# Three of eight output chunks finished on GpSimd, and eight stores in place of four

## The reference

```python
def rmsnorm(x, g):
    xf = x.astype(f32)
    y = xf * lax.rsqrt(jnp.mean(xf * xf, axis=-1, keepdims=True) + EPS)
    return y.astype(x.dtype) * g

def layer_step(x, ...):
    ...
    x = x + g1 * o
    x = x + g2 * hier_moe(modulate(rmsnorm(x, n2), sh2, sc2), ...)
    return x, new

    y_prompt = rmsnorm(xp, final_norm_g)
    y_sample = rmsnorm(xs, final_norm_g)
```

## Time and profile before

| | us |
|---|---|
| median of 3 runs | 781.53 (781.06 to 781.74) |
| span of the profiled execution, first to last instruction | 780.0 |
| TensorE busy | 740.1 (95%) |
| VectorE busy | 582.4 (75%) |
| ScalarE busy | 502.5 (64%) |
| GpSimd busy | 50.4 (6%) |
| last multiplication of the program ends | 770.60 |
| first of the eight scalings begins, the last ends | 772.93, 777.22 |
| first store issued, last store issued | 774.10, 777.25 |

### The profile page before, as it was taken

How to read it: one execution, slowest core, us unless ns; L and a number is a source line. 1 busy time by engine, 2 the same in 40 slices (tenths; PEclk the granted TensorE clock), 3 DMA queues, 4 the chain that set the end, 5 groups by cost and what they waited for, 6 DMA issues and landing times.

```text
span 780.0 us, 10973 instructions
## 1 busy us (share of the span) xinstructions
PE 740.1 (95%) x4020; PEld 573.8 (74%) x4020; DVE 582.4 (75%) x968; ACT 502.5 (64%) x834; POOL 50.4 (6%) x36
## 2 busy tenths in 40 slices
PE   4999999899999999999999999989999999999995
PEld 2557877458966788888768788755798788888874
DVE  3258386987565889999858746979766789998965
ACT  3049693584456877777746578557556887777852
POOL 0001342000000000000000125200000000000000
PEclk9999999999999999999999999999999999999998
DMA  9963034977238899999855112186741199999902
GB/s 366 425 244 109 11 124 155 424 274 289 103 116 350 317 377 356 363 366 381 312 232 184 55 55 70 67 355 235 287 149 55 55 328 376 378 364 376 368 20 84
DMA packets 33489, 186.26 MB, mean 239 GB/s; under 512 B 5136, under 2 KB 6288, under 8 KB 16400
## 3 DMA queue, kind: packets, MB, share of 16 engines
q1 hardware_dynamic: 33424, 185.42, 62.9%
HBM read 182.79 MB, written 2.62 MB: 238 GB/s over the span
## 4 chain that ended last, share of the span: by engine, by line
PE 77%; DVE 11%; ACT 7%; issue 4%; DMA 1%; DVEq 0%; ACTq 0%; SPq 0%
PE psum L877 23%; PE psum L906 11%; PE psum L1024 11%; PE psum L1226 5%; PE psum L991 4%; PE psum L707 3%; PE psum L929 3%; PE psum L855 2%; DVE att L2264 1%; PE psum L758 1%; PE psum L1196 1%; PE psum L743 1%; PE psum L1094 1%; ACT split L1419 1%; PE psum L890 1%
## 5 line engine op out<-in xcount | busy, mean ns | idle before, releaser
L2053 DVE TENSOR_TENSOR split<-ring,split 128x2048 fp32r<-128x2048 f32 x96 | 219.9, 2290 | 27.1 <-ACT split L1544 25.4
L1544 ACT CAST split<-ring 128x2048 fp32r<-128x2048 f32 x96 | 183.6, 1912 | 22.4 <-PE psum L906 14.5
L877 PE MATMUL psum<-split,y_hi 128*128 128x512 f32 x512 | 161.1, 396 | 0.4 <-ACT selT L1517 0.4
L877 PEld LDWEIGHTS psum<-split,y_hi 128*128 128x128 f32 x512 | 93.7, 188 | 18.7 <-issue 0.5
L877 PE MATMUL psum<-split,y_lo 128*128 128x512 f32 x256 | 100.2, 391 | 0.0
L1024 PE MATMUL psum<-ring_r,hT_hi 128*128 128x512 f32 x216 | 73.2, 393 | 0.0
L906 PE MATMUL psum<-split,hidT 128*128 128x512 f32 x256 | 69.7, 394 | 1.8 <-DVE hidT_lo L2058 1.8
L906 PEld LDWEIGHTS psum<-split,hidT 128*128 128x128 f32 x256 | 47.3, 188 | 14.1 <-DVE hidT_lo L2058 4.8
L877 PEld LDWEIGHTS psum<-split,y_lo 128*128 128x128 f32 x256 | 48.0, 188 | 10.4
L2495 POOL TENSOR_TENSOR ud<-const,da_hi 128x1024 fp32r<-128x1024 f32 x12 | 27.3, 2293 | 398.8 <-DVE da_lo L2154 391.3
L1024 PEld LDWEIGHTS psum<-ring_r,hT_hi 128*128 128x128 f32 x216 | 40.0, 188 | 9.0 <-issue 0.8
(11 more groups left out here) (314 smaller groups left out, 1426.3 us busy)
## 6 DMA issues: line engine op xcount, KB each, us to landing
ring<-in_w_gu SPq DMA_DIRECT2D x64, 1024.0 KB, 6.1
ring<-in_w_ada SPq DMA_DIRECT2D x40, 1024.0 KB, 7.0
ring<-in_w_down SPq DMA_DIRECT2D x32, 1024.0 KB, 6.2
ring<-in_w_rows SPq DMA_DIRECT2D x12, 1024.0 KB, 4.9
ring<-in_first SPq DMA_DIRECT2D x8, 1024.0 KB, 14.7
ring<-in_w_out SPq DMA_DIRECT2D x8, 1024.0 KB, 5.0
ring<-in_w_xbc SPq DMA_DIRECT2D x8, 800.0 KB, 9.2
par<-in_par SPq DMA_DIRECT2D x1, 1728.0 KB, 13.5
```

Source lines behind the costliest of these rows:

```text
L877: last = pe.matmul(dst, x[:, g, t, :], w[:, j, :], start=(t == 0 and i == 0), stop=(t == KD - 1 and i == 2))
L1544: act.copy(splits[unit_split(n)][:, 0, :], slot(key)).then_inc(raised("whi", l, p), 1)
L2053: tt(lo, slot(unit_key(l, p, n)), hi.bitcast(F32), ALU.subtract).then_inc(raised("wlo", l, p), 1)
```

## The change

ScalarE writes, for chunks 0, 1 and 2, x times the chunk's column of the gain into `hT`, one instruction behind each of these chunks' squares (`with_gain`). The final Exp writes `rstd` in SBUF and raises the bank's semaphore, as in layer 1. VectorE scales only the other five chunks, now with `rstd` as its factor. GpSimd waits for the bank's semaphore and multiplies the three prepared chunks by `rstd`, in place. SP issues eight stores of one chunk (192 KB) each, in the order 3, 4, 0, 5, 1, 6, 7, 2, each behind the wait for its chunk.

```diff
+LAST_POOL = (0, 1, 2)
+LAST_DVE = tuple(c for c in range(KD) if c not in LAST_POOL)
+LAST_OUT = (3, 4, 0, 5, 1, 6, 7, 2)
...
-            for c in range(0, KD, 2):
-                sp.wait_ge(*modulated(DEPTH, 0, c + 1))
-                sp.dma_start(a_out[0][:, c:c + 2, :], hT[:, c:c + 2, :]).then_inc(y_out, 16)
-            sp.wait_ge(y_out, 16 * KD // 2)
+            for c in LAST_OUT:
+                if c in LAST_POOL:
+                    sp.wait_ge(sig["hp"], LAST_POOL.index(c) + 1)
+                else:
+                    sp.wait_ge(sig["h"], KD + LAST_DVE.index(c) + 1)
+                sp.dma_start(a_out[0][:, c, :], hT[:, c, :]).then_inc(y_out, 16)
+            sp.wait_ge(y_out, 16 * KD)
...
+            def with_gain(c):
+
+                act.activation(hT[:, c, :], xT[:, c, :], ACT.Copy, scale=pcol[:, 2 * N_PROW + c:2 * N_PROW + c + 1])
+
...
                     act.activation(sq[:, c, :], xT[:, c, :], ACT.Square).then_inc(sig["sq"], 1)
+                    if l == DEPTH and c in LAST_POOL:
+                        with_gain(c)
...
-                if l in ROUNDED:
+                if l in ROUNDED or l == DEPTH:
                     act.activation(rstd, src[:, 0:TOK], ACT.Exp, scale=-0.5).then_inc(*was_read(key))
...
-                if l in ROUNDED:
+                if l in ROUNDED or l == DEPTH:
                     dve.wait_ge(*taken(key))
...
                 if l == DEPTH:
-                    src = bank(key)[:, 0:TOK]
-                    for c in range(KD):
-                        stt(hT[:, c, :], xT[:, c, :], pcol[:, 2 * N_PROW + c:2 * N_PROW + c + 1], src, ALU.mult, ALU.mult)\
+                    for c in LAST_DVE:
+                        stt(hT[:, c, :], xT[:, c, :], pcol[:, 2 * N_PROW + c:2 * N_PROW + c + 1], rstd, ALU.mult, ALU.mult)\
                             .then_inc(sig["h"], 1)
                     return
...
+            pool.wait_ge(*taken(("ss", DEPTH, 0)))
+            for c in LAST_POOL:
+                tt(hT[:, c, :], hT[:, c, :], rstd, ALU.mult).then_inc(sig["hp"], 1)
```

More of the change, by code:

```diff
@@ L539, in build @@
         for name, n in (
-                ("sq", 2 * KD), ("fold", 2), ("rstd", 1), ("h", KD), ("hx", 4), ("hx_hi", KD), ("hx_lo", KD), ("wx_hi", KD // 2), ("wx_lo", KD // 2), ("wx_spent", 1), ("shift_wr", 1), ("scaled", 2 * KD), ("roots", 2), ("rests", KD + 1), ("routed", KD - 1), ("conv", 6), ("xbc_silu", 6), ("dt_na", 1), ("dt_u", 1),
+                ("sq", 2 * KD), ("fold", 2), ("rstd", 1), ("h", KD), ("hp", len(LAST_POOL)), ("hx", 4), ("hx_hi", KD), ("hx_lo", KD), ("wx_hi", KD // 2), ("wx_lo", KD // 2), ("wx_spent", 1), ("shift_wr", 1), ("scaled", 2 * KD), ("roots", 2), ("rests", KD + 1), ("routed", KD - 1), ("conv", 6), ("xbc_silu", 6), ("dt_na", 1), ("dt_u", 1),
                 ("dt_r", 1), ("da", 1), ("bss", 3), ("brs", 3), ("prep", 3), ("ud", 3), ("ud_lo", 3), ("da_lo", 1), ("xd", 3), ("yx", 3),
@@ L1792, in _ @@
                                 act.activation(sq[:, c, :], xT[:, c, :], ACT.Square).then_inc(more_sig[l]["sq"], 1)
+                                if l == DEPTH - 1 and c in LAST_POOL:
+                                    with_gain(c)
                             act.preload_act_table_set("natural_log_exp_and_others")
```

## The result

The changed kernel takes 782.73 us (median of 20 runs, 781.14 to 783.81) against 781.47 (20 runs, 780.26 to 782.96): a ratio of 1.0016 with a 95% interval of 1.001 to 1.0023. It is slower by 1.26 us. That is the side that was forecast, inside the range of 780.7 to 783.0, but more than twice the 0.57 us of the sum. It lies 0.03 above the forecast's own bounds (781.7 to 782.7) and inside the range by the 0.3 that was added for scatter; whether the loss stays under 0.2% is not settled either, since the interval reaches 0.23%. The span of the profiled execution grew from 780.0 to 781.4.

What follows compares the result with a forecast made beforehand. TensorE, busy 740 of 780.0 us, was taken as the bound, leaving only the tail in reach. Alternating scalings and products, then stores, land last at 780.2 (+0.55); span about 780.6 plus 1.5 gives 782.1 us, range 780.7 to 783.0.

Steps and rivals of the forecast that it cites:

- the sum: Reckoning of the tail's turns and stores: last landing 780.2 against 779.65, +0.55; span about 780.6, median 782.1 us.
- the forecast's own bounds: Limits of the forecast case: 782.7 with GpSimd products at 1.04, 781.7 with cheaper turns and a last landing after 1.9.
- the 0.3 that was added for scatter: Allowance in us for the scatter of three runs, widening the range at both ends to 780.7 to 783.0.
- exclusion in alternation: Tail scalings: VectorE and GpSimd exclude one another instruction by instruction and take turns; 782.1 us, chance 0.84.
- the third rival: Tail: GpSimd keeps the ports for three products in a row, VectorE's other four scalings follow; 783.1 us, chance 0.06.
- The second rival: Tail: no exclusion worth the name, VectorE and GpSimd work side by side; gain 0.5, 781.0 us, chance 0.10.
- The forecast that ScalarE's products are free: Three 0.59 us products behind the squares of chunks 0 to 2 fit ScalarE's 0.86 idle: cost 0, upper bound 1.8.
- so VectorE begins first: Start of the tail: VectorE starts 0.03 after ScalarE's result, GpSimd 0.08; VectorE's first chunk ends at 773.56.
- The product: GpSimd's 384-column product in the tail, taken as 0.83 us, bounds 0.29 and 1.04.
- The bound of 1.04: Upper bound in us for one GpSimd product, from the 128x512 form; it would make the forecast 782.7.
- The pace of 0.46: SP's stores at the end: one ready store follows another at 0.46 us; last issue at 778.20.
- the engines are no limit: DMA engines in the tail: stores are issued slower than 0.53 us per 192 KB, so the engines don't set the end.

## Why the prediction was right, and where its size came from

The verdict (slower, by less than 0.2%) fits the medians, with the reservation made above on the 0.2%, and the mechanism held: exclusion in alternation, instruction by instruction, with VectorE's turn between two products, so the third rival fell at once; by the time alone its 783.1 was nearer to the 782.73 than the forecast, and it takes the timeline, where no scaling lasts over 1.45, to part the two. The second rival fell too, and the kernel with the factor in PSUM shows it by itself: there its picture, scalings 0.53 apart beside undisturbed products, came true, with a tail of 6.71 where its gain of 0.5 gives 6.57, so it was right about nearly everything but the operand on which it turns. The forecast that ScalarE's products are free held. The tail's growth of 1.33 divides along the experiments. The third step takes the order of the stores along with the exclusion: with the factor in PSUM the order costs nothing, since from its second store on SP waits for no chunk, and the second step lies within the reading error.

| step | from, to | us |
|---|---|---|
| eight stores in place of four | 7.07, 6.68 | -0.39 |
| three chunks to GpSimd, no exclusion | 6.68, 6.71 | +0.03 |
| exclusion | 6.71, 7.48 | +0.77 |
| stores that wait in the wrong order | 7.48, 8.40 | +0.92 |

The prediction was 0.8 short on the tail (7.6 by its own times, against 8.40): 0.62 in the last issue and 0.18 behind it. Three terms of its sum were mis-sized:

- **Who comes first.** The step "so VectorE begins first" failed. VectorE's scaling did start earlier, at 773.00 against 773.04, but GpSimd's product had the first turn: it took 0.99, as much as with no rival, and the scaling waited. The rows gave when an instruction starts, not when it gets its turn. Putting VectorE first takes 0.62 off the tail; that kernel gives it two turns ahead of the first product, where the sum had one, and no run has the sum's own order, so how much of the 0.8 this step is worth is not shown exactly.
- **The product.** 0.83 was read off a line through two forms with a broadcast operand; it takes 0.99 to 1.00 with two full ones. The bound of 1.04 held and was the better end of the two. In the alternation it is 1.27 from one product to the next, where 1.18 was reckoned, and VectorE's last result came 5.03 behind its start, not 4.76. The estimate of 0.84, worked out by proportion from the figure of the Trainium skill (GPSIMD Engine Reference, 3.1, Elementwise), which is for an addition of two inputs, is below what was measured as well.
- **The stores.** The pace of 0.46 was near (0.37 for the first that follows, then 0.49 or 0.50), but the sum had two stores in a row at the end, and there were five. That follows in the main from the first term: with GpSimd first, its chunks are ready early and the list has them late. The last issue came 5.87 behind the start, not 5.25. And "the engines are no limit" failed at the end: five stores in a row came faster than 0.53 apart, so the engines were full to 780.6, and the span ended 2.53 behind the last issue, not 2.35.

The rule of the Trainium skill (SBUF, State Buffer, Who interferes with whom) was borne out in its main part: the kernel whose scaling reads one SBUF tensor ran undisturbed, and with two each waited out the whole instruction of the other. That the one which issues first wins is not what the records show here, by 0.04 or 0.05 us; at 496 us in the earlier trace rows, where VectorE's record led by 0.06, VectorE did win.

## What to carry to other kernels

Before work is shared out between VectorE and GpSimd, look at where each operand lies: with two SBUF tensors on VectorE's side and a product of two SBUF tensors on GpSimd's the pair works as one engine, and a product that costs 0.99 there for 0.53 here is then a loss. A list of stores must follow the order in which the chunks really get ready, since one that isn't ready holds up those behind it; and when the DMA engines are nearly the bound, stores small enough to keep them filled are worth more than faster arithmetic.

## What the runs showed that was not expected

- GpSimd won the first turn in all three profiled executions in which both were released by the same semaphore, though VectorE's record began 0.04 or 0.05 earlier each time (773.00 and 773.04, 772.52 and 772.57, 771.55 and 771.59). Why was not settled: the records show when an instruction starts, not when it gets its turn.
- The turns between the two cost little. A waiting product loses 0.31 to a scaling that takes 0.61 alone and stands 0.53 from the next.
- 1.57 MB in stores of one chunk or of two moved at about the same rate from the engines' first byte to their last: some 367 GB/s in the kernel with eight stores, with packets of 1536 bytes, and 374 over the four larger stores.
